# First projections of a two-block transformer kernel: twelve pairs of output tiles, each by seven block products instead of eight

## Chip, cores and metric

One core of a Trainium2 chip. The metric is the time of one launch in device microseconds (us); lower is better.

## Reference

Two transformer blocks over 1024 tokens of width 1024, all in float32. The part that the change touches is the first projection of block one:

```python
h = rmsnorm(x, norm_mix[l])
proj = h @ w_in[l]        # (1024 x 1024) @ (1024 x 5664)
q, k, v, r, lr_f, lr_b, u, g_a, g_b = jnp.split(proj, split_points, axis=-1)
```

q and k (512 columns each), v and r (1024 each) are columns 0 to 3071 of `w_in`: 24 tiles of 128 columns. The two gate ranks `lr` are 32 columns from 3072 on, u, g_a and g_b the 2560 behind them. Gated linear attention over four heads, a pooling branch, an output projection and a feed-forward follow, then the second block.

## The kernel before

Everything lies feature-major: `acc[p, k, t]` holds feature `128*k + p` of token `t`, for eight `k`. A float32 product is made of three matmuls of rounded parts: an operand `a` is split into a high part (a rounded copy, type fp32r) and a low part (`a` minus the high part), and a product is hi*hi + hi*lo + lo*hi. For the first projection `h1hi` and `h1lo` are the parts of `x` times `norm_mix`, without the division by the root of the mean square, which is multiplied in afterwards as `rstd`.

A **unit** is one tile of 128 output columns for all 1024 tokens: 8 `k` times 3 parts times 2 token halves = 48 matmuls of 128x512 (`mm_unit`, L531). SP loads its weights into `raw` (L455, 512 KB), POOL makes `whi` (L497) and `wlo` (L501), PE multiplies into a pair of PSUM banks, DVE multiplies by `rstd` into `stage` (L654) and ACT's queue stores it to `proj` in memory (L659). `in_steps` runs units 0 to 24: tile 0, the `lr` columns (stored as tile 24), a loop of 22, tile 23. The other 20 units are spread over the four heads of the attention (`mid_unit`). `start_act` turns x into `acc` and spills it; `norm_act` and `norm_dve` make `h1hi` (L611), `h1lo` (L615), the squares (L546) and their sums (L557, L560), one `k` at a time, while PE runs unit 0 behind them. `norm_sum` (L567) sums over partitions, `norm_mean` (L594 to L579) makes a diagonal of it, `norm_spread` (L573) spreads it, `norm_root` (L604) is the square root. The order of work on each engine is the program's order; engines meet at semaphores only.

Behind the units, `gla_pe` starts with `z(0, 0)` (L876), a product of `lrT` (the `lr` rows loaded back from `proj`), then `mid_unit(0, 0)`; ACT and DVE meanwhile make the gates of head 0.

The two feed-forwards of the kernel already use seven products for eight. Two tiles of output columns by two halves of the tokens by two halves of the contraction are a 2x2 block product, and seven products of sums of blocks give it. A **product** there is 4 `k` times 3 parts = 12 matmuls of 128x512 (L3288), a **pair** (of tiles) is 84. For each pair POOL makes four sums of weight blocks (L3149, L3156, L3157, L3164), ACT the seven high parts (L3188), and POOL, there too, nearly all the low parts (L3198); high and low parts go round a ring of four buffers, so no high part may be written before the product four places earlier is done. ACT copies the first product out (L3297), DVE adds the others (L3304, L3311, L3320).

Of the kernel before, what the change touches and what calls it, by code (L numbers as in the profile page):

```python
# [54 lines left out]
N_IN = 45  # L55
# [139 lines left out]
class Step:  # L195
# [23 lines left out]
    def landed(self):  # L219
# [4 lines left out]
SEMS = ("p_norm pt_out w_hi w_split unit_done sq_done sq_added norm_sum norm_mean rstd_ready hi_ready lo_ready "  # L224
# [6 lines left out]
        "mla_loaded latent_hi rope_sin kr_copied vh_tok p_ready mixa_hi ang_step "  # L231
        "latent_lo cs_moved lat_loaded side_sq lat_sum lat_mean lat_rstd lat_normed q_copied q_a q_rope rs_inv mixa_lo s_stat "
        "vh_t s_ready pt_ready pv_ready gates_loaded conv_loaded mv_loaded "
        "f_log mq_stored qk_back qw_loaded c_made "
        "conv_silu mv_tok om_sig num_copied h_squared h_rstd h_scaled h_turned h_gated mixm_hi ml_consts "
        "m_step g_step conv_step st_w h_step mixm_lo am_t mv_t st_ready ho_ready "
        "y_scaled x_added out_t out_ev x3_turned x3_out").split()
# [12 lines left out]
         "kt_turned": ("yb_scaled", 8), "kw_made": ("o_sum", 8), "u_made": ("lat_sum", 4),  # L250
         "x3_last_spilled": ("mv_loaded", 64)}
# [3 lines left out]
            ("gla_loaded", 48), ("wpool_loaded", 16))  # L255
# [9 lines left out]
def two_block_kernel(nc, A, out):  # L265
# [20 lines left out]
    proj = dram("proj", (N_IN * P, T))  # L286
# [13 lines left out]
    with ctx:  # L300
# [240 lines left out]
        def norm_square(act, name, k, src):  # L541

            m = SQ_BASE[name] + k
            if m >= 2:
                act.wait_ge(S["sq_added"], m - 1)
            act.activation(stage[:, m % 2, :], src, ACT.Square).then_inc(S["sq_done"], 1)  # L546

        def norm_add(dve, name, k, src=None):

            m = SQ_BASE[name] + k  # L550
            sq = stage[:, m % 2, :] if src is None else src
# [67 lines left out]
        OPERAND = {"mix": 0, "mix2": 8}  # L619

        def norm_act(act, name, ready, g=None, hi=None, src=acc, nk=KT, dst=rstd):
# [5 lines left out]
            norm_root(act, name, dst[:, :])  # L627

        def norm_dve(dve, name, ready, g=None, hi=None, lo=None, src=acc, nk=KT):
# [4 lines left out]
            norm_mean(dve, name, nk)  # L634
# [104 lines left out]
        def in_steps(eng, do):  # L739


            do(eng, Step(0), 0, 0)
            do(eng, Step(1), LR0, 24)
            with eng.Fori(0, 11) as i:
                for j in range(2):
                    do(eng, Step(2 + j, 2, i), i * (2 * P) + (1 + j) * P, None, i * (2 * P) + (1 + j) * P)
            do(eng, Step(24), 23 * P, 23)

        def in_sp(sp):
            def do(e, u, c0, j, r0=None):  # L750
# [24 lines left out]

# [9 lines left out]
        MID0 = 25  # L785
# [18 lines left out]
        def gla_sp(sp):  # L804
            sp.wait_ge(S["x_spilled"], 16)
            sp.wait_ge(S["stored"][1], 16)
            sp.dma_start(lrT, proj[24 * P:24 * P + 32, :]).then_inc(S["gla_loaded"], 16)

            def qkv(h):
                if h:  # L810
                    sp.wait_ge(S["qk_weighted"], 8 * h)
                sp.dma_start(gq, proj[h * P:(h + 1) * P, :]).then_inc(S["qk_loaded"], 16)
                sp.dma_start(gk, proj[(4 + h) * P:(5 + h) * P, :]).then_inc(S["qk_loaded"], 16)
                if h:
                    sp.wait_ge(S["vt_ready"], 2 * h)
# [11 lines left out]
            for u in (MID0, MID0 + 1):
                mid_weights(sp, u)
            for i in range(2):
                sp.wait_ge(S["stored"][i], 16 * ((MID0 + 1 - i) // 2))  # L830
            for h in range(GH):
                for i in range(MIDS):
# [5 lines left out]
                    sp.dma_start(proj[u.c * P:(u.c + 1) * P, :], stage[:, u.par, :])\  # L838
# [3146 lines left out]
```

## Time and profile before

| what | value |
|---|---|
| median of 3 runs | 2748.24 us (2747.73 to 2749.09) |
| the profiled execution, its own time | 2749.12 us |
| its span | 2747.3 us |
| PE busy | 2642.3 us (96%), 12530 matmuls |
| POOL busy | 1266.4 us (46%) |
| DVE busy | 1733.2 us (63%) |
| ACT busy | 983.3 us (36%) |

A span is what the engines' records cover; the execution's own time is 1.8 us longer. PE's busy time counts overlapping matmuls once, so the "mean ns of one" of a matmul (some 390) is longer than the step from one to the next. PEld is the weight load of each matmul and lies under PE. DVE is VectorE, ACT ScalarE, POOL GpSimd, SPq and ACTq the queues that issue transfers.

### The profile page before, as it was taken

What the parts mean: (1) busy time and instruction counts of PE and PEld (TensorE: products, weight loads), DVE (VectorE), ACT (ScalarE), POOL (GpSimd) and SP (SyncE); (2) the same over time, 40 slices, a digit from 0 to 9 for tenths busy, and PEclk for the clock granted to TensorE, in tenths of its full rate; (3) what the DMA queues carried; (4) which work ended last, traced back from release to release, by engine and by line L of the source; (5) the groups of instructions that cost most, each with busy time, mean ns of one, the idle gap of its engine ahead of it and who ended that gap; (6) DMA issues with size and microseconds to landing.
All of it is one profiled execution on the core that took longest, in us unless ns stands there. A gap on an engine that the chain in (4) does not pass through costs nothing.

```text
span 2747.3 us, 32550 instructions
## 1 busy us (share of the span) xinstructions
PE 2642.3 (96%) x12530; PEld 2131.1 (78%) x12530; DVE 1733.2 (63%) x1925; ACT 983.3 (36%) x1354; POOL 1266.4 (46%) x767
## 2 busy tenths in 40 slices
PE   7999999999999999999999899989898999999998
PEld 5888788787778788888777688756786888877777
DVE  4111355565747766667889656666548766777887
ACT  4000333343223333334335211657445333434444
POOL 2343323223445888886333353241034988823331
PEclk9999999999999999999999999999999999999999
DMA  5223333324442333336633352401323545654543
GB/s 185 92 99 102 106 101 114 122 91 155 138 146 77 89 115 115 100 109 201 201 112 106 113 167 90 140 1 45 108 77 108 154 141 168 200 165 153 169 138 138
DMA packets 332499, 340.30 MB, mean 124 GB/s; under 512 B 18315, under 2 KB 254454, under 8 KB 332358
## 3 DMA queue, kind: packets, MB, share of 16 engines
q1 hardware_dynamic: 322790, 302.73, 35.5%
q10 hardware_dynamic: 9568, 35.66, 3.3%
q8 instruction: 93, 1.52, 0.2%
q14 instruction: 48, 0.39, 0.0%
HBM read 229.01 MB, written 108.30 MB: 123 GB/s over the span
## 4 chain that ended last, share of the span: by engine, by line
PE 51%; DVE 9%; issue 2%; DMA 2%; ACT 2%; POOL 1%; SPq 0%; DVEq 0%; ACTq 0%; POOLq 0%
PE ps L3288 35%; PE ps L531 8%; PE ps L2361 2%; DVE op_lo L3365 2%; PE ps L2384 1%; PE ps L2371 1%; DVE sw_lo L3198 1%; DMA op_raw<-hidden 1%; DVE acc L3609 1%; PE ps L2864 0%; DVE acc L1887 0%; DVE x L2308 0%; DVE acc L3616 0%; DMA x_block<-acc 0%; DVE op_lo L3268 0%
## 5 line engine op out<-in xcount | busy, mean ns | idle before, releaser
L3288 PE MATMUL ps<-op_hi,sw_hi 128*128 128x512 f32 x1769 | 693.5, 392 | 17.2 <-DVE op_lo L3365 9.9
L3288 PE MATMUL ps<-op_hi,sw_lo 128*128 128x512 f32 x1769 | 690.5, 390 | 0.0
L3288 PE MATMUL ps<-op_lo,sw_hi 128*128 128x512 f32 x1769 | 690.3, 390 | 0.0
L497 POOL TENSOR_TENSOR w_hi_t<-w_raw,ones 128x1024 fp32r<-128x1024 f32 (+1 forms) x85 | 163.5, 1926 | 714.5 <-PE ps L531 344.5
L3288 PEld LDWEIGHTS ps<-op_hi,sw_hi 128*128 128x128 f32 x1769 | 333.3, 188 | 98.0 <-issue 18.2
L3288 PEld LDWEIGHTS ps<-op_hi,sw_lo 128*128 128x128 f32 x1769 | 333.3, 188 | 70.0
L3288 PEld LDWEIGHTS ps<-op_lo,sw_hi 128*128 128x128 f32 x1769 | 333.2, 188 | 68.9 <-issue 0.5
L654 DVE TENSOR_TENSOR stage<-ps,rstd 128x1024 f32<-128x1024 f32 x62 | 75.8, 1222 | 355.3 <-PE ps L531 336.9
L3188 ACT ACTIVATE sw_hi<-sw_sumNone 128x512 fp32r<-128x512 f32 (+1 forms) x252 | 157.1, 624 | 333.8 <-PE ps L3288 252.5
L531 PE MATMUL ps<-h1hi,w_hi_t 128*128 128x512 f32 x720 | 229.6, 400 | 13.0 <-DVE h1lo L615 9.0
L3198 POOL TENSOR_TENSOR sw_lo<-sw_sumNone,sw_hi 128x512 fp32r<-128x512 f32 x138 | 213.5, 1557 | 34.4 <-ACT sw_hi L3188 34.3
L531 PE MATMUL ps<-h1lo,w_hi_t 128*128 128x512 f32 x720 | 223.3, 392 | 0.0
L531 PE MATMUL ps<-h1hi,w_lo_t 128*128 128x512 f32 x720 | 222.9, 391 | 0.0
L3149 POOL TENSOR_TENSOR sw_sumNone<-sw_raw 128x512 f32<-128x512 f32 (+1 forms) x63 | 113.4, 1799 | 234.7 <-DVE sw_lo L3198 211.8
L501 POOL TENSOR_TENSOR w_lo_t<-w_raw,w_hi_t 128x1024 fp32r<-128x1024 f32 (+1 forms) x85 | 216.3, 2547 | 6.2
L3188 ACT ACTIVATE sw_hi<-sw_raw 128x512 fp32r<-128x512 f32 (+1 forms) x189 | 117.4, 622 | 197.8 <-PE ps L3288 196.0
L3198 POOL TENSOR_TENSOR sw_lo<-sw_raw,sw_hi 128x512 fp32r<-128x512 f32 x109 | 159.3, 1462 | 53.8 <-ACT sw_hi L3188 53.8
L531 PEld LDWEIGHTS ps<-h1hi,w_hi_t 128*128 128x128 f32 x720 | 133.9, 189 | 48.1 <-issue 10.5
L531 PEld LDWEIGHTS ps<-h1lo,w_hi_t 128*128 128x128 f32 x720 | 136.0, 189 | 28.9
L531 PEld LDWEIGHTS ps<-h1hi,w_lo_t 128*128 128x128 f32 x720 | 136.0, 189 | 28.8
L3164 POOL TENSOR_TENSOR sw_sumNone<-sw_raw,sw_sumNone 128x512 f32<-128x512 f32 (+1 forms) x63 | 91.7, 1455 | 87.6 <-DVE sw_lo L3198 84.8
L3156 POOL TENSOR_TENSOR sw_sumNone<-sw_sumNone,sw_raw 128x512 f32<-128x512 f32 (+1 forms) x63 | 98.7, 1566 | 62.7 <-DVE sw_lo L3198 59.9
(434 smaller groups left out, 4636.2 us busy)
## 6 DMA issues: line engine op xcount, KB each, us to landing
op_raw<-hidden SPq DMA_DIRECT2D x42, 1024.0 KB, 8.7
w_raw<-in_w_in SPq DMA_DIRECT2D x60, 512.0 KB, 4.0
sw_raw<-in_w_ffn_in SPq DMA_DIRECT2D x44, 512.0 KB, 5.4
proj<-stage ACTq DMA_DIRECT2D x42, 512.0 KB, 2.6
hidden<-hidden_blocks SPq DMA_DIRECT2D x13, 1536.0 KB, 6.1
hidden<-hidden_blocks SPq DMA_DIRECT2D x14, 1280.0 KB, 5.0
sw_raw<-in_w_up SPq DMA_DIRECT2D x32, 512.0 KB, 8.3
sw_raw<-in_w_down SPq DMA_DIRECT2D x32, 512.0 KB, 5.2
```

The lines of the kernel that those rows point to most:

```text
L497: ins = pool.tensor_tensor(whi[:, u.par, s], raw[:, u.par, s], ones[:, 0:1].to_broadcast([P, n]), ALU.mult)
L501: ins = pool.tensor_tensor(wlo[:, u.par, s], raw[:, u.par, s], whi[:, u.par, s].bitcast(F32), ALU.subtract)
L531: mm = pe.matmul(out[:, b * HALF:(b + 1) * HALF], w, x[:, k, b * HALF:(b + 1) * HALF], start=(begin and k == ks[0] and n == 0), stop=(end ...
L654: dve.tensor_tensor(stage[:, u.par, :], PS[u.par if pair is None else pair][:, :], rstd[:, :], ALU.mult).then_inc(S["unit_out"][u.par], 1)
L2361: mm = pe.matmul(PS[n % 2][:, b:b + w], qT[0:96, h, i * P:(i + 1) * P], kT[0:96, h, b:b + w], start=True, stop=True)
L3149: pool.tensor_tensor(s1, a21, a22, ALU.add).then_inc(S["sw_sum"], 1)
L3156: pool.tensor_tensor(s2, s1, a11, ALU.subtract).then_inc(S["sw_sum"], 1)
L3164: pool.tensor_tensor(s2, a12, s2, ALU.subtract).then_inc(S["sw_sum"], 1)
L3188: act.activation(wshi[ring(m)][:, 0:n], weight_block(p, r), ACT.Copy).then_inc(S["sw_hi"], 1)
L3198: eng.tensor_tensor(wslo[ring(m)][:, 0:n], weight_block(p, r), wshi[ring(m)][:, 0:n].bitcast(F32), ALU.subtract).then_inc(S["sw_lo"], 1)
L3288: mm = pe.matmul(out, w, x[:, k, :], start=(k == 0 and i == 0 and r < 4), stop=(k == n - 1 and i == 2), skip_group_check=r >= 4)
L3365: dve.tensor_tensor(lo_of(first, r)[:, :, :], fresh_of(first, r)[:, :, :], hi_of(first, r)[:, :, :].bitcast(F32), ALU.subtract).then_inc(S ...
```

## The change

Only the `lr` columns stay a unit (unit 0, now first). The 24 tiles of q, k, v, r become twelve pairs (`IN_PAIRS`), each by seven products of 12 matmuls. The first two pairs are interleaved product by product in the order `IN_FIRST`; from the third pair on the products of a pair follow in order 0 to 6. Products 0, 4 and 6 use blocks of `h1hi`, `h1lo`; products 3, 1, 2, 5 need the block sums `t1` to `t4` of the activations with their high and low parts (`thi`, `tlo`), which DVE and ACT make once, while the first two pairs run. POOL makes the weight sums (`in_sum`) and, for products 2 and 3 of the sequence and all from number 14 on (the third pair), the low parts (`in_lo`, `POOL_LOW`); DVE makes the other low parts. ACT makes all high parts (`in_hi`), which POOL did in a unit. DVE's work on results is `in_post`: nine operations of 128x512 a pair. The `lr` rows go from PSUM to `lrT` directly (`lr_dve`), the stores move from ACT's queue to SP's, 256 KB each, and the weights of a pair are loaded as two transfers of 512 KB into `raw` (even pairs) or `stage` (odd ones). Squares of the first norm go to another place, since `stage` holds weights. `rmask`, `bm`, `gr` change places within `acc`. Nine semaphores of later stages are shared with new early ones, their counts shifted by constants (`count`).

```diff
+IN_PAIRS = [t for h in range(GH) for t in ((h, 4 + h), (8 + 2 * h, 9 + 2 * h), (16 + 2 * h, 17 + 2 * h))]
+IN_ORDER = (0, 1, 2, 3, 4, 5, 6)
+IN_FIRST = (0, 4, 3, 1, 2, 5, 6)
+IN_SEQ = [(p, r) for r in IN_FIRST for p in range(2)] + [(p, r) for p in range(2, N_INP) for r in IN_ORDER]
...
+        def in_pair_load(sp, p):
...
+            if p == 0:
+                sp.wait_ge(S["w_split"], 1)
+            if p >= 2:
+                sp.wait_ge(S["in_lo"], IN_AT[p - 2, 6] + 1)
...
+        def in_hi(act, m):
+            p, r = IN_SEQ[m]
+            act.wait_ge(*in_landed(p))
+            if r in IN_SUM_OF:
+                act.wait_ge(S["in_sum"], IN_SUM[p, IN_SUM_OF[r]])
+            if m >= 4:
+                act.wait_ge(S["in_product"], m - 3)
+            elif m >= 2:
+                act.wait_ge(S["unit_done"], U_IN + 1)
+            act.activation(in_ring(whi, m), in_block(p, r), ACT.Copy).then_inc(S["in_hi"], 1)
+        POOL_LOW = (2, 3) + tuple(range(14, N_IN_SEQ))
...
         def in_pool(pool):
-            in_steps(pool, lambda e, u, c0, j, r0=None: split_unit(e, u))
+            split_unit(pool, Step(U_IN))
+            for m in POOL_LOW[:2]:
+                in_lo(pool, m)
+            pool.wait_ge(S["x_spilled"], 16)
+            pool.wait_ge(S["t_fresh"], 1)
+            for which in (1, 2, 3, 4):
+                for p in range(2):
+                    in_sum(pool, p, which)
+            for p in range(2, N_INP):
+                for which in (1, 3, 2):
+                    in_sum(pool, p, which)
+                for r in IN_ORDER:
+                    in_lo(pool, IN_AT[p, r])
+                    if r == 1:
+                        in_sum(pool, p, 4)
...
+        def in_product(pe, m):
...
+            if r == 5:
+                pe.wait_ge(S["in_post"], IN_POST[p, "u3"])
+            if r == 6:
+                pe.wait_ge(S["in_post"], IN_POST[p, "22"])
...
+            pe.wait_ge(S["in_lo"], m + 1)
+            if r in T_OF:
+                pe.wait_ge(S["lo_ready"], KT + T_OF[r] + 1)
...
         def in_pe(pe):
+            mm_unit(pe, Step(U_IN), h1hi, h1lo, to=PS[3], wait_k=lo_wait(pe, "mix"))
+            norm_sum(pe, "mix", KT, ps=1)
+            for m in range(N_IN_SEQ):
+                if m == 3:
+                    norm_spread(pe, "mix", ps=1)
+                in_product(pe, m)
...
         def in_act(act):
+            for m in range(4):
+                in_hi(act, m)
+            in_first(act, 0)
+            t1_gained(act)
+            in_first(act, 1)
+            t_hi(act, 0)
+            in_hi(act, 4)
+            in_hi(act, 5)
+            norm_root(act, "mix", rstd[:, :], ps=1)
+            t_hi(act, 1)
+            in_hi(act, 6)
+            in_hi(act, 7)
+            t_hi(act, 2)
+            in_hi(act, 8)
+            in_hi(act, 9)
+            t_hi(act, 3)
...
         def in_dve(dve):
+            in_lo(dve, 0)
+            in_lo(dve, 1)
+            t1_dve(dve)
+            norm_mean(dve, "mix", KT, ps=1)
+            t2_dve(dve)
+            t_lo(dve, 0)
+            in_lo(dve, 4)
+            t34_dve(dve, 0)
+            in_lo(dve, 5)
+            t_lo(dve, 1)
+            lr_dve(dve)
+            in_lo(dve, 6)
+            in_lo(dve, 7)
+            t_lo(dve, 2)
+            in_lo(dve, 8)
+            t34_dve(dve, 1)
+            in_lo(dve, 9)
+            t_lo(dve, 3)
+            for m in range(6, N_IN_SEQ):
+                for what in in_posts(*IN_SEQ[m]):
+                    in_post(dve, IN_SEQ[m][0], what)
+                if m + 4 < N_IN_SEQ and m + 4 not in POOL_LOW:
+                    in_lo(dve, m + 4)
...
         def mid_pool(pool):
             for u in range(MID0, N_IN):
+                if u < MID0 + 2:
+                    pool.wait_ge(S["in_product"], N_IN_SEQ - 2 if u == MID0 else N_IN_SEQ)
                 split_unit(pool, Step(u))
```

## Rows read from the trace of the kernel before

**Rows 1.** Part 1 of the page: busy us (share of the span) xinstructions.

```profile
PE 2642.3 (96%) x12530; PEld 2131.1 (78%) x12530; DVE 1733.2 (63%) x1925; ACT 983.3 (36%) x1354; POOL 1266.4 (46%) x767
```

**Rows 2.** Busy time by stretch; behind PEclk the DMA share and GB/s.

```profile
60.00:300.00 240.00, 240.00 (x1061) 198.72 (x1060) 27.58 (x23) 0.00 (x0) 95.05 (x45) 1.00 0.33 110
904.00:1260.00 356.00, 355.71 (x1562) 294.48 (x1563) 241.67 (x247) 112.94 (x188) 309.64 (x207) 1.00 0.36 106
325.00:330.00 5.00, 2.31 (x11) 2.31 (x12) 4.63 (x4) 3.13 (x4) 0.00 (x0) 0.78 0.06 26
```

**Rows 3.** Timeline of DVE, projection stage: start us, us, what, [idle before <-releaser].

```profile
70.65 1.23 DVE L654 TENSOR_TENSOR stage<-ps,rstd 128x1024 f32<-128x1024 f32 x1 [9.75 <-PE ps L531]
...
288.25 1.23 DVE L654 TENSOR_TENSOR stage<-ps,rstd 128x1024 f32<-128x1024 f32 x1 [9.75 <-PE ps L531]
```

**Rows 4.** Timeline of POOL, first feed-forward, from one pair to the next.

```profile
998.55 1.74 POOL L3149 TENSOR_TENSOR sw_sumNone<-sw_raw 128x512 f32<-128x512 f32 x1
...
1003.20 1.30 POOL L3198 TENSOR_TENSOR sw_lo<-sw_raw,sw_hi 128x512 fp32r<-128x512 f32 x1
...
1017.59 1.74 POOL L3149 TENSOR_TENSOR sw_sumNone<-sw_raw 128x512 f32<-128x512 f32 x1
```

**Rows 5.** Groups by line, stretch 904 to 1260 us (the first feed-forward).

```profile
L3288 PE MATMUL ps<-op_hi,sw_hi 128*128 128x512 f32 x521 | 203.3, 390 | 2.1 <-DVE s_u L3311 2.1
L3198 POOL TENSOR_TENSOR sw_lo<-sw_sumNone,sw_hi 128x512 fp32r<-128x512 f32 x75 | 114.5, 1535 | 19.3 <-ACT sw_hi L3188 19.3
L1678 DVE TENSOR_TENSOR hidden_blocks<-hidden_blocks,rstd 128x512 f32<-128x512 f32 x40 | 48.5, 1247 | 0.0
L3188 ACT ACTIVATE sw_hi<-sw_sumNone 128x512 fp32r<-128x512 f32 x75 | 47.5, 633 | 112.9 <-PE ps L3288 82.1 <-POOL sw_sumNone L3156 28.8 <-issue 2.0
L3320 DVE TENSOR_TENSOR hidden_blocks<-ps,s_u 128x512 f32<-128x512 f32 x55 | 37.8, 688 | 46.0 <-PE ps L3288 46.0
L3149 POOL TENSOR_TENSOR sw_sumNone<-sw_raw 128x512 f32<-128x512 f32 x19 | 32.7, 1721 | 0.5 <-DMA sw_raw<-in_w_ffn_in 0.5
```

**Rows 6.** Timeline of the start, 22 to 53 us.

```profile
22.50 1.89 POOL L497 TENSOR_TENSOR w_hi_t<-w_raw,ones 128x1024 fp32r<-128x1024 f32 x1
22.68 2.79 DVE L615 SCALAR_TENSOR_TENSOR h1lo<-acc,cols,h1hi 128x1024 fp32r<-128x1024 f32 x1 [22.68 <-ACT h1hi L611]
24.47 3.24 POOL L501 TENSOR_TENSOR w_lo_t<-w_raw,w_hi_t 128x1024 fp32r<-128x1024 f32 x1
25.39 2.87 DVE L557 COPY ssq<-stage 128x1024 f32<-128x1024 f32 x1
...
42.17 1.28 DVE L615 SCALAR_TENSOR_TENSOR h1lo<-acc,cols,h1hi 128x1024 fp32r<-128x1024 f32 x1
43.36 1.22 DVE L560 TENSOR_TENSOR ssq<-ssq,stage 128x1024 f32<-128x1024 f32 x1
...
46.68 0.30 PEld L531 LDWEIGHTS ps<-h1hi,w_hi_t 128*128 128x128 f32 x2
...
50.91 1.88 PE L573 MATMUL ps<-ssq,ones 128*128 128x512 f32 x4
```

**Rows 7.** All instructions of one line: duration ns min/median/max, first and last start.

```profile
L3365 DVE TENSOR_TENSOR op_lo<-op_raw,op_hi x49: 1751/2284/3355, 1267.8 to 2669.3; 128x2048 fp32r<-128x2048 f32 x42, 128x1536 fp32r<-128x1536 f32 x7
L579 DVE TENSOR_TENSOR ssq<-ident,bytok x4: 1227/2412/3269, 47.4 to 2099.6; 128x1024 f32<-128x1024 f32 x4
```

**Rows 8.** Transfers from issue to landing, projection stage, then first feed-forward.

```profile
w_raw<-in_w_in SPq DMA_DIRECT2D x23, 512.0 KB, 3.9
```

```profile
sw_raw<-in_w_ffn_in SPq DMA_DIRECT2D x36, 512.0 KB, 6.8
```

**Rows 9.** Timeline of PE where it had stood idle for 3 us in head 0.

```profile
322.74 1.91 PE L892 MATMUL ps<-ident,acc 128*128 128x128 f32 x16
...
327.69 3.68 PE L905 MATMUL ps<-qs,ks 128*128 128x128 f32 x16 [3.04 <-DVE ks L1142]
```

**Rows 10.** Timeline where the stage hands over to the attention.

```profile
309.80 1.98 PE L876 MATMUL ps<-ssq,wup 32*128 32x512 f32 x4
309.91 1.23 DVE L654 TENSOR_TENSOR stage<-ps,rstd 128x1024 f32<-128x1024 f32 x1 [9.65 <-PE ps L531]
```

More of the change, by code:

```diff
@@ L54 @@
 U_IN = 0
-N_IN = 45
+N_IN = 21
+N_PROJ = 45
 U_YA = U_IN + N_IN
@@ L82 @@
     LANDED.append(_c[_u % 2])
+    if _u == U_IN:
+        _c = [_n + 32 * (len(IN_PAIRS) // 2) for _n in _c]
 ORDER = (0, 1, 2, 3, 4, 5, 6)
@@ L545, in norm_square, with squares @@
                 act.wait_ge(S["sq_added"], m - 1)
-            act.activation(stage[:, m % 2, :], src, ACT.Square).then_inc(S["sq_done"], 1)
+            act.activation(squares(name)[m % 2], src, ACT.Square).then_inc(S["sq_done"], 1)
+        def squares(name):
+            if name == "mix":
+                return [fresh[3][:, 2 * i:2 * i + 2, :].rearrange("p a t -> p (a t)") for i in range(2)]
+            return [stage[:, i, :] for i in range(2)]
         def norm_add(dve, name, k, src=None):
             m = SQ_BASE[name] + k
-            sq = stage[:, m % 2, :] if src is None else src
+            sq = squares(name)[m % 2] if src is None else src
             n = NORM_AT[name]
@@ new lines, in t_hi, with t1_gained @@
+        def t_hi(act, i):
+            if i == 0:
+                act.wait_ge(S["t_gained"], 1)
+            else:
+                act.wait_ge(S["t_fresh"], i + 1)
+            act.activation(thi[i][:, :, :], (t1, t2, t3, t4)[i][:, :, :], ACT.Copy).then_inc(S["hi_ready"], 1)
+        def t1_gained(act):
+            act.wait_ge(S["t_fresh"], 1)
+            for k in range(4):
+                ins = act.activation(t1[:, k, :], t1[:, k, :], ACT.Copy, scale=col("norm_mix", k))
+            ins.then_inc(S["t_gained"], 1)
@@ new lines, in t1_dve, with t2_dve @@
+        def t1_dve(dve):
+            dve.tensor_tensor(t1[:, :, :], part(acc, 0, 1), part(acc, 0, 0), ALU.subtract).then_inc(S["t_fresh"], 1)
+        def t2_dve(dve):
+            dve.wait_ge(S["t_gained"], 1)
+            for k in range(4):
+                ins = dve.scalar_tensor_tensor(out=t2[:, k, :], in0=part(acc, 1, 1)[:, k, :],
+                                               scalar=col("norm_mix", 4 + k), in1=t1[:, k, :],
+                                               op0=ALU.mult, op1=ALU.subtract)
+            ins.then_inc(S["t_fresh"], 1)
@@ new lines, in t34_dve @@
+        def t34_dve(dve, i):
+            if i == 0:
+                dve.wait_ge(S["t_fresh"], 2)
+            else:
+                dve.wait_ge(S["lo_ready"], KT + 2)
+                dve.wait_ge(S["t_fresh"], 3)
+            for k in range(4):
+                ins = dve.scalar_tensor_tensor(out=(t3, t4)[i][:, k, :], in0=part(acc, i, 0)[:, k, :],
+                                               scalar=col("norm_mix", 4 * i + k), in1=t2[:, k, :],
+                                               op0=ALU.mult, op1=ALU.subtract)
+            ins.then_inc(S["t_fresh"], 1)
@@ L823, in gla_sp @@
             for i in range(2):
-                sp.wait_ge(S["stored"][i], 16 * (10 - i))
-            qkv(0)
+                sp.wait_ge(S["stored"][i], IN_STORED)
             gate(0)
[L827 to L830, printed above, removed]
             for h in range(GH):
```

271 lines of the change are left out of this document (213 added, 58 removed).

## The prediction, made before the changed kernel ran

> **What bounds the kernel now.** I read the page's busy shares first, then busy time by stretch, the timelines of the stage, and last the same views of the first feed-forward, which already works in the way that the change brings here. PE is busy 96% of the span [rows 1]: the kernel is bound by how many matmuls PE has to run, and what saves matmuls saves time unless PE is made to wait. From 60 to 300 us, the stage that changes, PE is busy in all 240.00 us at full clock; POOL works 95 us, DVE 28, ACT none [rows 2]. The evictions of units show the pace: from 70.65 to 288.25 us are 20 units, 217.60 / 20 = 10.88 us each [rows 3], 0.2267 us a matmul.
>
> The first feed-forward is the model of the changed stage. There PE is busy 355.71 of 356.00 us at full clock [rows 2], and POOL's first sum of one pair and of the next start 19.04 us apart [rows 4]; 84 matmuls at 0.2267 are 19.04. So a matmul costs the same in both forms, and a pair paid by seven products runs there with no wait that counts.
>
> **What the change saves.** Two units take 21.76 us, a pair 19.04: 2.72 saved (12 matmuls), 12 times: 32.6 us. The `lr` unit stays whole.
>
> **From the third pair on: is it covered?** POOL has 4 sums and 7 low parts a pair. In the feed-forward POOL did the same eleven at 1.54 us a low part and up to 1.72 a sum [rows 5], about 17.3 us of 19.04, with PE fed. Here DVE is quieter: nine operations a pair, six of them with one input in PSUM (0.69 us each [rows 5]), three (`22s`, `21s`, `12s`) with both in SBUF (1.25). That is about 7.9 us, while DVE was busy 241.67 of 356 there [rows 2], 12.9 a pair. ACT: 7 high parts and a copy at 0.63 [rows 5], 5 us. The tightest turn is the change of pair. The high part of product 6 of pair p may start when product 2 is done (ring of four); behind it POOL queues its low part, three sums and the low part of the next pair's product 0, which PE wants 4 products (10.9 us) later. ACT 0.63, low parts 2 times 1.54, sums 3 times 1.6: 8.5 us; 10.9 - 8.5 leaves 2.4. At 1.74 for all five [rows 4] it is 9.3, still covered. Weights: the load of pair p+2 is issued when the last low part of p is made and is wanted a whole pair later, against 6.8 us to land [rows 8]. SP's queue holds it behind the stores of the pair before, whose last waits for product 6 and its scaling: under a pair's time too. Cost: 0.
>
> At one place a rule speaks against giving POOL the low parts. The row first: a DVE subtraction of 128x2048 takes 2.28 us in the median and 3.36 at worst [rows 7], and DVE operations on PSUM stay at 0.69 beside a busy POOL [rows 5]. The Trainium skill (SBUF — State Buffer, "Who interferes with whom") says that a DVE instruction with two SBUF inputs and a POOL instruction that reads SBUF exclude each other for their whole length, and that DVE with at most one SBUF input is free of it. By that rule the three `s` operations would each hold POOL up by 0.65 us, 2 us a pair, still under PE's 19.04; the trace agrees with it as far as the rows go.
>
> **The start, before the first product: a gain.** Before, POOL's split of the second unit (22.50 to 27.7) ran beside DVE's first two operations, which took 2.79 and 2.87 us [rows 6] in place of about 1.28 and 1.22 as later. In the changed kernel POOL splits only the `lr` unit first, which was done by 22.5, and has nothing more to do till the high parts 2 and 3. DVE's chain, which PE follows, is earlier by 1.5 + 1.6 = 3.1 us; I take 3.0. First product: 46.7 - 3.0 = 43.7 us (46.68 before [rows 6]). The bound below is 0, if the earlier load of pair 1 (1 MB) or the low clock of PE there takes it back.
>
> **The first two pairs: a loss.** 14 products at 2.72 are 38.1 us, and the spread 1.3: PE alone would be at the third pair at 83.1. DVE's list: low parts 0 and 1 (0.66 each), t1 (2.2), mean and diagonal (0.4 + 1.23, 3.27 beside POOL [rows 6, 7]), t2 (4 of 0.66), t_lo(0) (2.2 [rows 7]), and so on to t_lo(3): 26.8 us without POOL. It begins at 41.5 (44.6 before, less 3). Two waits on ACT are in it: t2 waits for `t1_gained`, which stands in ACT's queue behind the copy of product 0 (done at 46.4; ready about 49.6), and t_lo(3) waits for t_hi(3), 2.1 us. POOL's eight sums run beside most of it, 1.2 to 1.6 us each, and each can hold a DVE operation up by its own length (3.28 for 2.20, rows 7): 6 to 10 us. So DVE is done with t_lo(3) at 76.7 to 80.2. PE meanwhile does products 0 to 9 with waits of 1.4 (t_lo(0)), 0.6 and 1.4 us and is done at about 76.2. Product 10 (number 5 of pair 0) needs `t4` and the operation `u3`, which stands in DVE's queue behind t_lo(3), two `u2` and two low parts: 3.4 us more, 80.1 to 83.6. That is a PE wait of 4 to 7 us, the largest of the change. After an idle of 3.04 us PE ran 16 small matmuls in 3.68 us where 16 took 1.91 before [rows 9], at a mean clock of 0.78 [rows 2], so between its two levels of 2.4 and 1.2 GHz: 1.8 us lost, of which 1 counts here since product 11 waits for DVE anyhow (seven more operations of DVE, 83.5 to 87). Products 11 to 13 end at 91.6 to 95.
>
> Then the third pair. Its weights go where pair 0's were, and may be loaded only when low part 12, DVE's ninth operation behind t_lo(3), is made: 82.8 to 86.4. Two transfers land 5 to 7 us later [rows 8], then come three sums and a low part on POOL, 5.2 us: its first product starts at 94.5 to 97.6. I take 96.0: 12.9 us behind the 83.1. By 19.04 us a pair, ten pairs follow with no wait.
>
> **The hand-over.** z(0, 0) followed the last unit at once [rows 10]. Its new waits (`21` of the last pair; `lrT` long made) end during product 6. The first two units' weights are loaded in pair 10; POOL can split the first once product 82 is counted, 4.3 us of the 5.5 that PE still runs. DVE had an eviction of 1.23 there [rows 10], now 0.69 + 0.66. gv is loaded during the last pair and wanted 13 us into the attention. Cost 0; if gv were late, up to 3 us.
>
> **The sum.** 32.6 + 3.0 - 12.9 = 22.7 us. The profiled execution took 2749.1, the median of the runs is 0.9 lower: 2749.1 - 22.7 - 0.9 = 2725.5, say **2726 us**. Bounds: the start's gain 0 to 3; the first pairs' loss 8 (sums of POOL and DVE never meet, weights land in 4 us) to 17 (each meets, a second fall of the clock); hand-over 0 to 3. Best 32.6 + 3 - 8 = 27.6 (2720.6); worst 32.6 - 17 - 3 = 12.6 (2735.6).
>
> **Rivals.**
> 1. The start costs nothing, because DVE's waits and PE's overlap more than I reckoned: 32.6 + 3.0 less 2 at most, 33.6, 2714.6. For it: over the whole feed-forward stretch PE waited for DVE's sums 2.1 us in all [rows 5]. Against it: there the operands were partly made before, here `t4` and its low part come last on one engine. Chance 0.08.
> 2. POOL sets the pace from the third pair on. With every operation at the 1.74 of rows 4, eleven are 19.1 us, and the waits at the ring come on top: 20 us a pair, 10 us more in all, 2736. For it: POOL has only 10% to spare. Against it: the feed-forward ran so with a busier DVE. Chance 0.09.
> 3. Slower than before: the change of pair becomes a stall on each pair. Once POOL's five operations between product 2 and the next product 0 pass 10.9 us (2.05 us each), PE stands, and from about 3 us of idling it also loses its clock (1.8 us, rows 9): 19.04 + 3 + 1.8 = 23.8 a pair, 10 times 4.8 = 48 more than forecast, 2774. It outweighs the gain from a pair time of 19.04 + 2.27 = 21.3 on. Against it: no POOL group of this size is over 1.8 us in the mean. Chance 0.03.
> That the change saves no matmuls is excluded by its text: 84 for 96.
>
> **How the numbers follow.** Forecast 0.80, rivals 0.08, 0.09, 0.03. The range leaves out rival 1's best and rivals 2 and 3 beyond 2735: 2716 to 2735. A difference of 0.2% (5.5 us) is about what a measurement can tell from no change. Faster by more needs under 2742.7: the forecast and rivals 1 and 2, 0.96; within 0.2% 0.01; slower 0.03.
>
> **What the profile after would show.** Right: about 12,386 matmuls (144 fewer), first product at about 44 us, one wait of PE of 4 to 7 us near 77 us put down to DVE, a second of 1 to 4 us near 93 ended by POOL, then pairs 19.04 us apart with PE never idle, z(0, 0) at about 287 us in place of 309.8. Wrong: a PE wait at each change of pair (rival 3), POOL over 95% busy between 100 and 286 (rival 2), or a new wait in head 0.

## The result and the profile after

The changed kernel takes 2720.52 us in the median of four runs (2716.09 to 2726.63), the kernel before 2747.98; the ratio is 0.9901, with a 95% interval from 0.9882 to 0.9921. That is 27.5 us less. The forecast was 22.7 less (2726, from 2716 to 2735), so the time lies in the range, 5.5 us under the forecast. The profiled execution took 2716.09 us, the fastest of the four; its span is 2714.4.

Part 1 of the page after, to be read beside [rows 1]:

```profile
PE 2605.7 (96%) x12386; PEld 2100.2 (77%) x12386; DVE 1820.3 (67%) x2038; ACT 1050.4 (39%) x1458; POOL 1342.9 (49%) x839
```

PE has 12,386 matmuls, 144 fewer, as forecast. Busy time by stretch after (us of PE, PEld, DVE, ACT, POOL, then granted clock, DMA share, GB/s), beside [rows 2]:

```profile
60.00:80.00 20.00, 18.37 (x72) 14.51 (x72) 18.62 (x21) 9.83 (x11) 8.93 (x2) 0.91 0.00 1
80.00:100.00 20.00, 16.63 (x65) 13.27 (x66) 13.74 (x21) 3.11 (x6) 9.47 (x7) 0.91 0.55 160
100.00:280.00 180.00, 180.00 (x796) 149.05 (x795) 69.63 (x85) 45.80 (x75) 143.30 (x104) 1.00 0.38 117
```

From 100 to 280 us PE never stands, at full clock, while POOL is busy 143.30 of 180 us, or 15.2 a pair, and DVE 7.4. Everything that was lost is lost before 100 us. There the timeline of PE has these waits (in brackets the idle time before the instruction and what ended it):

```profile
54.70 0.50 PE L953 MATMUL ps<-h1hi,w_hi_t 128*128 128x512 f32 x1 [1.41 <-ACT acc L972]
...
60.51 0.50 PE L953 MATMUL ps<-op_hi,w_hi_t 128*128 128x512 f32 x1 [2.81 <-DVE w_lo_t L907]
...
81.92 0.50 PE L953 MATMUL ps<-op_hi,w_hi_t 128*128 128x512 f32 x1 [3.04 <-DVE acc L1065]
...
82.89 0.63 PE L953 MATMUL ps<-op_hi,w_hi_t 128*128 128x512 f32 x1
83.32 0.63 PE L953 MATMUL ps<-op_lo,w_hi_t 128*128 128x512 f32 x1
...
96.17 0.47 PE L953 MATMUL ps<-h1hi,w_hi_t 128*128 128x512 f32 x1 [1.44 <-DVE acc L1065]
...
286.77 1.98 PE L1185 MATMUL ps<-ssq,wup 32*128 32x512 f32 x4
```

The waits are before products 3, 4, 10 and 14, the last being the first of the third pair. The lines at 82.89 and 83.32 are 0.43 us apart, where a matmul at full clock takes 0.23: PE ran at 1.2 GHz for a time behind the wait at 81.92. The last line is z(0, 0), 23.0 us earlier than in [rows 10]. From 96.17 to 286.77 are ten pairs, 19.06 us each. DVE after, at the start and where it feeds products 4 and 10, beside [rows 6]:

```profile
22.63 1.28 DVE L658 SCALAR_TENSOR_TENSOR h1lo<-acc,cols,h1hi 128x1024 fp32r<-128x1024 f32 x1 [22.63 <-ACT h1hi L654]
23.84 0.69 DVE L600 COPY ssq<-op_raw 128x1024 f32<-128x1024 f32 x1
...
49.25 4.72 DVE L1017 SCALAR_TENSOR_TENSOR op_raw<-acc,cols,op_raw 128x512 f32<-128x512 f32 x4 [2.50 <-ACT op_raw L984]
56.48 2.30 DVE L1038 TENSOR_TENSOR op_lo<-op_raw,op_hi 128x2048 fp32r<-128x2048 f32 x1 [2.52 <-ACT op_hi L979]
58.71 1.75 DVE L907 TENSOR_TENSOR w_lo_t<-acc,w_hi_t 128x512 fp32r<-128x512 f32 x1
...
68.17 2.27 DVE L1038 TENSOR_TENSOR op_lo<-op_raw,op_hi 128x2048 fp32r<-128x2048 f32 x1
...
70.98 2.72 DVE L1030 SCALAR_TENSOR_TENSOR op_raw<-acc,cols,op_raw 128x512 f32<-128x512 f32 x4
...
75.69 3.19 DVE L1038 TENSOR_TENSOR op_lo<-op_raw,op_hi 128x2048 fp32r<-128x2048 f32 x1 [1.38 <-ACT op_hi L979]
...
81.19 1.48 DVE L1065 TENSOR_TENSOR acc<-ps,acc 128x512 f32<-128x512 f32 x2
...
83.91 0.68 DVE L907 TENSOR_TENSOR w_lo_t<-acc,w_hi_t 128x512 fp32r<-128x512 f32 x1
```

The first two operations, 2.79 and 2.87 us before, take 1.28 and 0.69 with POOL at rest. t2 (49.25) takes 4.72 us beside POOL's sums; t_lo(3) ends at 78.88, and `u3`, which product 10 waits for, is the first half of the line at 81.19. Low part 12 (83.91) releases the load of the third pair. POOL after:

```profile
56.60 3.31 POOL L884 TENSOR_TENSOR acc<-stage 128x512 f32<-128x512 f32 x1
67.78 7.68 POOL L888 TENSOR_TENSOR acc<-w_raw,acc 128x512 f32<-128x512 f32 x1 [7.87 <-DVE w_lo_t L907]
75.43 1.29 POOL L888 TENSOR_TENSOR acc<-stage,acc 128x512 f32<-128x512 f32 x1
90.39 1.50 POOL L871 TENSOR_TENSOR acc<-w_raw 128x512 f32<-128x512 f32 x1 [13.67 <-DMA w_raw<-in_w_in]
...
94.81 1.26 POOL L907 TENSOR_TENSOR w_lo_t<-w_raw,w_hi_t 128x512 fp32r<-128x512 f32 x1
...
106.68 1.29 POOL L871 TENSOR_TENSOR acc<-stage 128x512 f32<-128x512 f32 x1
...
125.72 1.29 POOL L871 TENSOR_TENSOR acc<-w_raw 128x512 f32<-128x512 f32 x1
```

The third pair's weights land at 90.39, 5.8 us behind low part 12; three sums and a low part follow, done at 96.07, and PE starts at 96.17. The view names DVE as what ended that wait, but DVE's operation ended at 95.46: it was POOL's. Later pairs are 19.04 us apart (106.68 to 125.72).

So the stage gave what was forecast, 23.0 us for 22.7. The span of this execution is 32.9 us shorter, though: 9.9 us more appear behind z(0, 0), in stages whose instructions the change leaves alone. The experiments ask two things: what the four waits hang on, and where those 9.9 us come from.

### The profile page after: what moved, and what is told of

The parts are those of the page before. It is cut to its first block, busy times and chain, and to the rows that moved or that the text cites. A ratio compares the mean times of both kernels' runs of the same rounds, so it can differ in the third digit from the quotient of the medians.

```text
span 2714.4 us, 32479 instructions
## 1 busy us (share of the span) xinstructions
PE 2605.7 (96%) x12386; PEld 2100.2 (77%) x12386; DVE 1820.3 (67%) x2038; ACT 1050.4 (39%) x1458; POOL 1342.9 (49%) x839
## 4 chain that ended last, share of the span: by engine, by line
PE 53%; DVE 9%; issue 2%; ACT 2%; POOL 1%; DMA 1%; DVEq 0%; SPq 0%; ACTq 0%; POOLq 0%
PE ps L3600 36%; PE ps L568 10%; DVE op_lo L3677 2%; PE ps L2673 2%; PE ps L2696 1%; DVE sw_lo L3510 1%; PE ps L2683 1%; PE ps L3176 1%; DVE acc L3921 1%; DVE acc L3928 1%; DVE x L2620 0%; DVE op_lo L3580 0%; PE ps L3561 0%; DVE x L2632 0%; DVE sq_sum_a L2132 0%
## 5 line engine op out<-in xcount | busy, mean ns | idle before, releaser
L534 POOL TENSOR_TENSOR w_hi_t<-w_raw,ones 128x1024 fp32r<-128x1024 f32 (+1 forms) x61 | 119.0, 1954 | 536.2 <-DMA w_raw<-in_w_in 261.5
L538 POOL TENSOR_TENSOR w_lo_t<-w_raw,w_hi_t 128x1024 fp32r<-128x1024 f32 (+1 forms) x61 | 158.0, 2595 | 4.3
L695 DVE TENSOR_TENSOR stage<-ps,rstd 128x1024 f32<-128x1024 f32 x37 | 45.1, 1220 | 126.1 <-PE ps L568 110.8
L3632 DVE TENSOR_TENSOR hidden_blocks<-ps,s_u 128x512 f32<-128x512 f32 x111 | 76.1, 686 | 78.2 <-PE ps L3600 77.7
L3677 DVE TENSOR_TENSOR op_lo<-op_raw,op_hi 128x2048 fp32r<-128x2048 f32 (+1 forms) x49 | 118.9, 2428 | 7.5 <-ACT op_hi L3670 7.5
L3616 DVE TENSOR_TENSOR s_u<-ps,s_p 128x512 f32<-128x512 f32 x65 | 44.8, 689 | 115.4 <-PE ps L3600 109.9
L568 PE MATMUL ps<-h1hi,w_hi_t 128*128 128x512 f32 x336 | 109.9, 408 | 11.3 <-DVE h1lo L658 7.4
L568 PE MATMUL ps<-m2hi,w_hi_t 128*128 128x512 f32 x304 | 106.3, 405 | 4.1 <-DVE m2lo L1310 2.1
L568 PE MATMUL ps<-h1lo,w_hi_t 128*128 128x512 f32 x336 | 104.6, 393 | 0.0
```

Of the source, the lines that this page charges most:

```text
L534: ins = pool.tensor_tensor(whi[:, u.par, s], raw[:, u.par, s], ones[:, 0:1].to_broadcast([P, n]), ALU.mult)
L538: ins = pool.tensor_tensor(wlo[:, u.par, s], raw[:, u.par, s], whi[:, u.par, s].bitcast(F32), ALU.subtract)
L568: mm = pe.matmul(out[:, b * HALF:(b + 1) * HALF], w, x[:, k, b * HALF:(b + 1) * HALF], start=(begin and k == ks[0] and n == 0), stop=(end ...
L3632: dve.tensor_tensor(out, bank(p, r), u[:, :], ALU.add).then_inc(S["s_post"], 1)
L3677: dve.tensor_tensor(lo_of(first, r)[:, :, :], fresh_of(first, r)[:, :, :], hi_of(first, r)[:, :, :].bitcast(F32), ALU.subtract).then_inc(S ...
```

## The experiments

Since the start of an execution shifts by up to 2 us from run to run (the first product of the changed stage began between 42.84 and 45.34 us in eleven profiles), the stage is compared by its own length, first product to z(0, 0): 263.1 us before (46.7 to 309.8, [rows 6, 10]), 243.6 in the changed kernel. PE's waits and that length in each profile:

| kernel | waits of PE, us | first product to z(0, 0), us | median, us |
|---|---|---|---|
| changed | 1.41, 2.81, 3.04, 1.44 | 243.6 | 2720.5 |
| again | 1.42, 2.80, 3.01, 0.55 | 243.9 | 2720.9 |
| low_dve | 1.41, 2.79, 3.02, 2.56 | 244.6 | 2721.8 |
| better | 2.47, 1.90, 1.12, 0.73, 0.72 | 241.9 | 2717.4 |
| dve_order | 1.36, 2.80, 0.24, 0.96, 4.06 | 244.4 | 2719.4 |
| sum_first | 1.40, 2.80, 0.22, 0.94, 3.04, 0.72 | 243.2 | 2719.9 |
| early_load | 1.41, 2.81, 0.24, 0.96, 3.07 | 241.9 | 2717.6 |
| best | 2.47, 1.77, 0.95, 1.81 | 242.1 | 2718.6 |
| sums_late | 2.47, 3.32, 1.61, 0.31, 2.68 | 246.5 | 2721.5 |
| twice2 (one run) | 1.44, 2.80, 1.91, 0.30, 2.72 | 245.5 | 2727.3 |
| twice4 (one run) | 1.42, 2.80, 0.24, 0.95, 3.02, 3.11, then about 1 a pair | 259.4 | 2737.3 |

**again**: the changed kernel, unaltered.

> The changed kernel once more, unaltered. Seen so far: in its profiled execution z(0, 0) starts 23.0 us earlier than before (my forecast 22.7), but the span is 32.9 us shorter; the other 9.9 us appear one by one behind waits of PE in stages that the change doesn't touch (near 795, 904, 1313, 1500, 1766 and 2420 us). Theory A (falls of the clock): at those waits PE's granted clock falls or doesn't from one execution to the next, so the first 310 us repeat within 0.5 us, z(0, 0) again starts 23.0 to 23.4 us earlier, and the gain behind it comes out differently, anywhere from 0 to 10 us; the median of five rounds is 2718 to 2725. Rival B (a lasting effect of the change on later stages): the 9.9 us come again at the same places, and the time is 2716 within 1 us.

The stage repeats: 243.9 us for 243.6, with the same first three waits. The wait before product 14 is 0.55 us for 1.44, because PE ran slower just before it (mean clock 0.66 from 80 to 90 us, 0.83 in the first profile), and the third pair starts 53.2 us behind the first product, for 53.0. Median 2720.85 (2719.63 to 2721.84), ratio to before 0.9893 (0.9877 to 0.9910). Behind z(0, 0) this execution took 2431.8 us (2719.1 - 287.35), the first profile 2427.6, the kernel before 2437.5. So the gain there is not the same in each execution, as theory A has it: 9.9 us in the first profile, 5.7 in this one. Where the two differ can be seen in busy time by stretch, from the first profile and then from this one:

```profile
770.00:780.00 10.00, 9.78 (x43) 8.11 (x44) 2.34 (x3) 0.73 (x1) 4.41 (x3) 1.00 0.50 160
```

```profile
770.00:780.00 10.00, 10.00 (x39) 8.10 (x38) 2.58 (x3) 1.02 (x2) 3.50 (x2) 0.83 0.52 160
```

In both, PE has just stood 2.0 us for one weight unit, until 770.23 in the first and 769.34 in the second. In the first profile the clock stays at its level of 2.4 GHz; in the second, part of the stretch ran at 1.2 GHz (0.83 in the mean), and though PE was busy for all of it, it did 39 matmuls where the first did 43. The loss is 10.00 × (1 - 0.83), 1.7 us.

**late1**: the kernel before, with one more sum over partitions at the first norm. That is eight matmuls of 128x128 in the program and 16 more records in the profile (12,546 for 12,530); the 64 of the expectation is wrong, its 1.7 us is not: PE is busy 3.73 us there instead of 1.95.

```diff
                 if first:
+                    e.wait_ge(S["sq_added"], SQ_BASE["mix"] + KT)
+                    for _ in range(1):
+                        sum_tokens(e, 3, [ssq])
                     norm_sum(e, "mix", KT)
```

> The kernel before with 64 matmuls of 128x128 (1.7 us of PE) put ahead of the sum of the first norm; their result isn't used. It moves everything behind it by 1.7 us and changes nothing else. Theory A (later falls of the clock depend on when a wait comes): the time differs from 2748.0 + 1.7 = 2749.7 by 1 us or more either way, and the difference sits behind waits of PE in later stages. Rival B: all later stages just move by 1.7 us, 2749.7 within 0.7.

Ten runs gave 2745.71 to 2754.05, median 2750.26; thirteen runs of before beside them 2747.55 to 2752.40, median 2749.31. In its profile z(0, 0) starts 2.5 us later than before (312.3; 1.8 us are the added matmuls, 0.7 the shift of the start), and the span is 2747.5 against 2747.3: the 2.5 us have gone again behind z(0, 0). Two of the ten runs were faster than any of before (2746.15 and 2745.71), three slower than all of them (2753.33 to 2754.05): they spread over 8.3 us, those of before over 4.9. This fits theory A. The medians do not decide it: they are 0.95 us apart, and the interval of the ratio (0.9993 to 1.0012, or -1.9 to +3.3 us) holds a mere shift too.

Summed over each profile behind z(0, 0), as PE's busy time times what is missing of the full clock in stretches of 10 us: 15.6 us lost in before, 13.4 in late1, 9.6 in the first profile of the change, 12.4 in again, 12.7, 10.7, 11.7, 13.2, 8.7, 13.7 and 14.5 in low_dve, better, dve_order, sum_first, early_load, best and sums_late, 18.4 in twice2, 12.9 in twice4. The time behind z(0, 0) less this loss and less PE's idle time (up to its last matmul) is 2345.8 to 2348.1 us in all thirteen, the kernel before 2347.0 and the changed one 2346.2: little else differs. Of the 9.9 us of the first profile 6.0 are clock (15.6 - 9.6), 3.1 idle time of PE (74.9 - 71.8). That part is a lasting gain: PE's idle time is 71.0 to 72.6 us in ten of the eleven profiles of a changed kernel (74.6 in best), 74.9 in before and 74.6 in late1. The largest piece of it, in the timeline of PE before, then after, is a wait for one of the output projection's weight units:

```profile
794.89 0.78 PE L531 MATMUL ps<-m1hi,w_hi_t 128*128 128x512 f32 x2 [3.25 <-POOL w_lo_t L501]
```

```profile
770.23 0.73 PE L568 MATMUL ps<-m1hi,w_hi_t 128*128 128x512 f32 x2 [2.01 <-POOL w_lo_t L538]
```

This wait was 3.25 us in before and 3.24 in late1, and 1.96 to 2.41 in all eleven profiles of a changed kernel. POOL starts on these weights 14.95 us behind the issue of their transfer before (775.58 to 790.53) and 13.70 after (752.15 to 765.85): the 1.25 us are the landing. Nothing in the program says why; the cause stays open.

**low_dve**: the low parts from the third pair on by DVE.

```diff
-        POOL_LOW = (2, 3) + tuple(range(14, N_IN_SEQ))
+        POOL_LOW = (2, 3)
...
                 for r in IN_ORDER:
-                    in_lo(pool, IN_AT[p, r])
```

> DVE instead of POOL makes the low parts of the weights from the third pair on. Theory A (PE sets the pace from there on, and who makes the low parts is indifferent): DVE has 9 operations and 7 low parts of 0.7 to 1.3 us a pair, 13 to 17 us, pairs stay 19.04 us apart, the time is the changed kernel's within 2 us. Rival B (the helper's turn at the change of pair counts): pairs lengthen by 0.5 to 2 us, as DVE's queue puts low parts behind operations that wait for PE, 5 to 20 us more in all.

Busy time from 100 to 280 us in this kernel:

```profile
100.00:280.00 180.00, 180.00 (x796) 149.10 (x795) 107.67 (x152) 46.46 (x76) 46.42 (x36) 1.00 0.40 123
```

DVE is busy 107.67 us, POOL 46.42, and PE 180.00 as in the changed kernel: 2721.8 us, ratio 0.9897 (0.9881 to 0.9914). Theory A: which of the two makes the low parts is worth nothing from 100 us on, and about 1 us in all (244.6 for 243.6 and 243.9, a wait of 2.56 before product 14). The seven cost DVE 4.0 us a pair (38.0 more in 180 us, or 9.45 pairs) and POOL 10.2 (96.9 less).

**twice2 and twice4**: two or four low parts of each pair from the third on made twice; the diff is that of twice2, twice4 has r in (0, 2, 4, 5).

```diff
                 for r in IN_ORDER:
+                    if r in (2, 5):
+                        m = IN_AT[p, r]
+                        pool.wait_ge(S["in_hi"], m + 1)
+                        pool.tensor_tensor(in_ring(wlo, m), in_block(p, r), in_ring(whi, m).bitcast(F32), ALU.subtract).then_inc(S["low_again"], 1)
+                        pool.wait_ge(S["low_again"], len((2, 5)) * (p - 2) + (2, 5).index(r) + 1)
                     in_lo(pool, IN_AT[p, r])
```

> Low parts of products 2 and 5 made twice on POOL in each pair from the third on: 2 operations of 1.3 us more a pair; results unchanged. POOL was busy 143.3 us of 180 in the changed kernel, 15.2 a pair. Theory A (POOL's room is what its busy time leaves, 3.9 us a pair): 17.9 us of 19.04, pairs stay 19.04 us apart, at most 0.3 more. Rival B (the waits at the ring leave less room than that): over 19.5 us a pair.

> The same with four low parts of a pair (products 0, 2, 4, 5) made twice: POOL 15.2 + 5.4 = 20.6 us a pair. Theory A: POOL sets the pace, pairs are 20.6 to 21.5 us apart, and ten pairs cost 16 to 25 us, so that most of the change's gain is gone. Rival B (part of POOL's time is only DVE holding it, which slack takes up): below 20 us a pair.

Busy time of twice2 from 100 to 280 us, and PE's timeline in twice4 at two changes of pair:

```profile
100.00:280.00 180.00, 180.00 (x793) 148.94 (x792) 68.40 (x83) 46.72 (x76) 167.65 (x124) 1.00 0.37 116
```

```profile
138.77 0.47 PE L958 MATMUL ps<-h1hi,w_hi_t 128*128 128x512 f32 x1 [1.07 <-DVE acc L1070]
...
159.39 0.47 PE L958 MATMUL ps<-h1hi,w_hi_t 128*128 128x512 f32 x1 [0.97 <-DVE acc L1070]
```

With two more, POOL is busy 93% and PE still never waits; the ten pairs take 192.2 us for 190.6 only because the clock was down behind the wait of 2.72 us before the first of them (mean 0.64 from 96.51 to 100.00 us). With four, pairs are 20.62 us apart (138.77 to 159.39), PE stands about 1 us at each change of pair, and z(0, 0) comes 15.8 us later than in the changed kernel (259.4 - 243.6). POOL's room is its idle time, 3.9 us a pair, to within a few tenths; theory A in both, though the ten pairs cost 14.1 us more (204.7 for 190.6), not 16 to 25, as the first of them is hardly slower. The waits of about 1 us cost no clock (PE's clock is 1.00 from 100 to 280 us).

**sum_first**: in the third pair POOL makes low part 14 behind one sum.

```diff
+            in_sum(pool, 2, 1)
+            in_lo(pool, IN_AT[2, 0])
+            in_sum(pool, 2, 2)
+            in_lo(pool, IN_AT[2, 1])
+            in_sum(pool, 2, 3)
...
```

> Of the three changes of order, POOL's order in the third pair alone (low part 14 behind one sum, not three). Theory A: in the changed kernel POOL's low part 14 was made at 96.07, PE could have begun at 94.7; PE's wait of 1.4 us there goes and nothing more is gained, since DVE's queue sets product 10 to 13: 1.4 us or less. Rival B (landing and sums set it): 2.5 us or more.

The wait of 1.44 at product 14 goes and 0.72 comes back two products later, where the sum put behind is wanted: 243.2 for 243.6. Theory A.

**dve_order**: DVE does `u2` and low part 10 ahead of t_lo(3), `u3` behind it, low parts 12 and 13 ahead of the scalings; ACT makes high part 10 ahead of t_hi(3).

```diff
+            in_hi(act, 10)
             t_hi(act, 3)
...
             in_lo(dve, 9)
+            in_post(dve, 0, "u2")
+            in_lo(dve, 10)
             t_lo(dve, 3)
...
+            in_post(dve, 0, "u3")
+            in_post(dve, 1, "u2")
+            in_lo(dve, 11)
+            in_post(dve, 0, "22")
+            in_post(dve, 1, "u3")
+            in_lo(dve, 12)
+            in_lo(dve, 13)
...
```

> Of the three changes of order, DVE's (with ACT's high part 10 ahead of t_hi(3)) alone. Theory A (the wait before product 10 is the queue of DVE behind t_lo(3)): that wait, 3.0 us in the changed kernel, falls below 1 us and product 10 starts 2.5 to 3 us earlier; the third pair starts only 1 to 1.5 us earlier, since its weights (landed 5.8 us behind low part 12) and three sums set it; the attention starts 1 to 2 us earlier. Rival B (t4's own making sets product 10): below 1 us gained at product 10.

The wait at product 10 is gone, so that step of theory A is right: it was the place in DVE's queue. But the third pair then waited 4.06 us for its weights, three sums and low part 14 (done at 94.62), and the clock fell behind that. Busy time by stretch:

```profile
90.00:100.00 10.00, 5.94 (x16) 4.36 (x16) 2.15 (x3) 1.67 (x3) 9.60 (x8) 0.70 0.78 236
```

At a mean clock of 0.70 the ten pairs from 94.72 on end at 288.14, 193.4 us for 190.6. The third pair starts 2.0 us earlier behind the first product (51.0 for 53.0) and its ten pairs take 2.8 longer, so the stage is 0.8 us longer than in the changed kernel, not 1 to 2 shorter. The expectation missed that.

**early_load**: third and fourth pair loaded when low part number 5 and the fourth sum of the pair two before are made.

```diff
-            if p >= 2:
+            if p in (2, 3):
+                sp.wait_ge(S["in_sum"], IN_SUM[p - 2, 4])
+                sp.wait_ge(S["in_lo"], IN_AT[p - 2, 5] + 1)
+            elif p >= 2:
                 sp.wait_ge(S["in_lo"], IN_AT[p - 2, 6] + 1)
```

> The earlier load alone, in the changed kernel. Theory A: the third pair starts when PE is done with product 13 (1.4 us earlier, 94.7 for 96.2), no more, since the wait before product 10 stays 3.0: first product to z(0, 0) 242.2 us for 243.6. Rival B: the wait there stays.

The wait at product 14 is gone and the stage takes 241.9 us, 1.7 less, as theory A said (242.2). Median 2717.6 (2712.75 to 2721.39).

**sums_late**: POOL's first sums wait for t2.

```diff
-            pool.wait_ge(S["t_fresh"], 1)
+            pool.wait_ge(S["t_fresh"], 2)
```

> POOL's sums of the first two pairs wait till t2 is made; nothing else altered. In the changed kernel t2 took DVE 4.72 us beside three sums. Theory A (POOL and DVE hold each other up, as in the forecast's 6 to 10 us): t2 takes 2.7 us, PE's wait of 1.4 us before product 3 goes, but the held-back sums meet t_lo(0), low part 4 and t3 instead, and PE waits about 2 us there: 0 to 1.5 us gained. Rival B (t2 is as long without the sums): nothing moves.

DVE's timeline in this kernel, t2 and then t3:

```profile
49.35 2.74 DVE L1017 SCALAR_TENSOR_TENSOR op_raw<-acc,cols,op_raw 128x512 f32<-128x512 f32 x4 [2.49 <-ACT op_raw L984]
...
58.50 5.81 DVE L1030 SCALAR_TENSOR_TENSOR op_raw<-acc,cols,op_raw 128x512 f32<-128x512 f32 x4
```

t2 takes 2.74 us for 4.72, and PE's wait at product 3 goes; but t3, 2.73 us in the changed kernel, now takes 5.81, since the sums meet it, and the wait goes to product 5 (3.32 us). What one gained the other lost, and the clock fell behind the new wait: 246.5 us, 2.9 longer. Theory A's mechanism holds, its sum was too hopeful.

**better and best**: sum_first, dve_order and sums_late together; best adds early_load.

> Three changes of order in the first three pairs: POOL's sums wait till t2 is made; DVE does u2 and low part 10 before t_lo(3) and u3 right behind it, and low parts 12 and 13 before the scalings; POOL makes low part 14 after one sum of the third pair instead of three. Theory A (what was lost there is the order of DVE's and POOL's queues, as forecast): PE's waits before products 3, 4 and 10 go from 1.4, 2.8 and 3.0 us to about 0, 2 and 0.5, the fall of the clock behind them goes too, and the third pair starts 3 to 4.5 us earlier, near 92 us; 2.5 to 4 us less than the changed kernel in the median, but for the clock's later falls. Rival B (the loading of pair 2's weights sets the start of the third pair, so order helps nothing): the third pair starts at 95 us or later, less than 1.5 us gained.

> The three changes of order together (as in the run called better) and one more: the weights of the third and fourth pair are loaded when low part number 5 of the pair two before and its fourth sum are made, not number 6, which reads no weight. In the changed kernel that moment is 80.1 us, against 84.6. Theory A (with the queues in order, the start of the third pair hung on the landing of its weights only): PE's waits behind product 5 of the sequence, 1.1 + 0.7 + 0.7 us in better, all go; first product to z(0, 0) takes 241.9 - 2.5 = 239.4 us; median 2.5 us under better, about 2715. Rival B (POOL's sums, not the landing, held it): less than 1 us gained over better.

better: 241.9 us for the stage, third pair at 92.54; 2717.4 us in the median (2716.03 to 2720.23), ratio 0.9885 (0.9868 to 0.9901), 3.4 less than the changed kernel beside it, of which the stage has 1.9 (241.9 for 243.9). The start of the third pair and the median are as theory A has them; the waits before products 4 and 5 (2.47 and 1.90) are not gone. best: 242.1 us and 2718.6. The weights land 6 us sooner there, low part 14 is made at 86.3, and PE still waits 1.81 us at product 14, by the timeline of PE:

```profile
93.02 0.50 PE L967 MATMUL ps<-h1hi,w_hi_t 128*128 128x512 f32 x1 [1.81 <-DVE acc L1082]
```

and by that of DVE:

```profile
91.32 1.05 DVE L1067 TENSOR_TENSOR acc<-acc,rstd 128x512 f32<-128x512 f32 x1
92.29 0.68 DVE L1082 TENSOR_TENSOR acc<-ps,acc 128x512 f32<-128x512 f32 x1
```

It waits for `12` of pair 0 (92.29), which frees the bank, and which stands behind the scalings that dve_order put last; DVE has had no idle moment since 58 us. Neither theory of that run was right: with landing and sums out of the way DVE's queue is next, its order or its sheer amount of work; no run separates the two. better, early_load and best cannot be told apart; all are 2 to 4 us faster than the changed kernel (2720.5 and 2720.9, only the latter run beside better), which is about what separates runs of one kernel.

## Why the prediction was right, and where it was off

- **Pace and saving.** 19.04 us a pair, 2.72 saved on each, 32.6 us: measured 19.06. POOL took 15.2 us a pair, not 17.3, with low parts at 1.29 to 1.40 us in the mean in place of 1.54. DVE is quieter here than in the feed-forward (busy 39% against 68% [rows 2]), which is the likely reason; no run tests it. Rival 2 (POOL sets the pace) fell: two operations more a pair do not bring it (twice2), four do (twice4).
- **The start.** 3.0 us forecast, 3.5 measured from DVE's first operation to the first product (24.0 before, 20.5 after); the copy was even shorter than I took it (0.69 for 1.22).
- **The first two pairs.** Forecast: t_lo(3) done at 76.7 to 80.2, product 10 at 80.1 to 83.6, third pair at 94.5 to 97.6. Measured: 78.88, 81.92 and 96.17. The loss behind the first product is 13.6 us (96.17 - 43.15 - 38.1 - 1.3) for 12.9. Inside it I missed one wait: the copy of product 0 of pair 1 (ACT) waits for t2, since it overwrites what t2 reads, so product 3 waited 1.41 us; and product 4 waited 2.81, not 1.4. The wait at product 10 was 3.04 in turn, not 4 to 7. And there were two falls of the clock, not one: matmuls are 0.43 us apart in place of 0.23 from 62.01 to 65.37 and from 82.89 to 85.88, about 1.6 us each. The four waits and the two falls are 11.9 of the 13.6 us. Neither set the start of the third pair. The first cost nothing: in dve_order, sum_first and early_load the clock stayed up there, PE waited 0.22 to 0.24 and 0.94 to 0.96 us instead, and product 6 began 24.6 us behind the first product in all three as in the changed kernel (67.74 - 43.15). The second was mostly waited for anyway, since low part 12, the landing and POOL's sums set product 14: in again PE ran slower still ahead of it, its wait there shrank from 1.44 to 0.55, and the third pair started only 0.2 us later (53.2 for 53.0). That the sum of 12.9 came within 0.7 us is in part luck: a wait at product 10 set too long and waits ahead of it set too short nearly cancel.
- **The hand-over.** 0 forecast; z(0, 0) came 190.6 us behind the third pair, ten pairs to 0.2 us, and the first wait in head 0 is 2.72 us for 3.04 [rows 9].
- **The sum.** 32.6 + 3.5 - 13.6 = 22.5, with 0.5 in rounding and the hand-over 23.0 at z(0, 0), for 22.7. The rest of the distance to 27.5 is a term that the sum did not have: behind z(0, 0) I took the kernel as unchanged. Its instructions are, its waits are not quite: one is 0.8 to 1.3 us shorter in each profile of a changed kernel, all of PE's idle time there about 3 us less in ten of eleven, and the falls of the clock at the other waits came to 6.0 us less in the one profile than in the one of before. That such falls come and go with the same instructions, again shows (one weight unit's wait, two clocks); late1 fits it. Why the changed kernels lose less to them in most profiles (8.7 to 14.5, and 18.4 in twice2, against 15.6 and 13.4) is not settled; with two profiles of the old stage it may be chance, and the medians, 28.5 us apart in the second set against 22.4 at z(0, 0), say that some of it is not.
- **Rivals.** 1 (no cost at the start) fell: the cost was 13.6. 3 (a stall on every pair) fell: no wait at all from 100 to 280 us. Its "about 3 us of idling" for a fall of the clock was read from one row and is too long: the clock also fell behind waits of 2.0 us (again, 769 us) and 1.81 us (best, 93 us).

## What to carry to other kernels

Where another stage of the same kernel already runs in the form that a change brings, its pace could be carried over to the tenth of a microsecond here; the work lies in the first turn, where the operands are made, and there the order of the queues decides which wait comes next, so that moving one wait alone mostly moves the loss. The helper engine had as much room as its idle time, which doubling some of its operations, until the bound engine waits, measures directly. A fall of the clock costs only where PE is the engine that the others wait for. Compare a stage by its own length, and give what comes behind it several profiles before it is called a gain.

## What the runs showed of the hardware

- **DVE in a row keeps POOL out.** POOL's fourth sum of pair 0 took 7.68 us (67.78), its twin right behind it 1.29. It is 7.67 to 7.76 us in all eleven profiles. DVE ran operations with two SBUF inputs back to back until 74.30 and was not held up itself (t_lo(2) 2.27 us, t4 four times 0.68); the sum ended 1.2 us behind the last of them. The Trainium skill (SBUF — State Buffer, "Who interferes with whom") says that a DVE instruction with two SBUF inputs contends with a GpSimd instruction that reads SBUF, and that the issue order decides which of the two blocks. The trace agrees that they exclude each other, and adds that POOL did not get its turn here between two of DVE's instructions. In another place it did: the sum at 56.60 ended 1.1 us behind t_lo(0) (59.91 and 58.78), and DVE's low part 4 (58.71), 0.68 us elsewhere, took 1.75. Which of the two comes next when both stand ready, no run settles. At 49.25, where POOL came first, t2 was the one held up (4.72 for 2.74 us).
- **The clock behind a wait.** After PE had stood 2.0 us (770 us) the granted clock fell from 2.4 to 1.2 GHz for a part of the next 10 us in one execution and stayed in another of the same program, 0.83 against 1.00. At product 10 of the changed kernel the low clock added 1.6 us to PE's own work; where nothing else held PE, it cost 1.6 us behind the wait of 2.72 in twice2 and 2.8 us behind that of 4.06 in dve_order (ten pairs in 192.2 and 193.4 us for 190.6). Falls are the likely reason why a kernel whose instructions are fixed spreads over 10.5 us here: the run of 2716.09 us has a mean granted clock of 0.992, that of 2726.63 one of 0.988, and 0.004 of 2720 us is 10.9 us, an estimate from rounded figures.
